# Streaming the tokens of the last product's tiles 2 to 7 in other orders

## The chip, the cores and the metric

The kernel runs on one core of a Trainium2 chip. The metric is the device time of one launch in microseconds (us); lower is better.

## The reference, cut to what matters

Two transformer-like blocks follow each other on 512 tokens of width 1024, all in float32. The change lies in the last product of the second block, the down projection of its feed-forward part. The lines that matter:

```python
ffn = (silu(u2 @ w_ffn_gate) * (u2 @ w_ffn_up)) @ w_ffn_down   # 2816 -> 1024 wide
h = h + gate2 * ffn
return rms_norm_2(h, final_g)
```

## The kernel before

**Layout.** Activations lie transposed: 128 features on the partitions, the 512 tokens side by side in the free dimension. A weight matrix is cut into blocks of 128 x 128. An output tile is 128 features x 512 tokens of float32, which is one whole PSUM bank.

**Precision.** Each float32 operand is split into a rounded part ("hi") and a rest ("lo"), both of a type (fp32r) that TensorE multiplies in one pass. A block is then three matmuls into the same bank: weight hi by activation hi (line 725), weight lo by activation hi (line 726), weight hi by activation lo (line 728). Each is one instruction that holds 128 x 128 weights and streams 512 columns, one for each token. The stationary operand is the weight block; the moving operand is the activation pair `act2`, the product of the two halves of the feed-forward part.

**Weights.** They come in units of eight blocks (512 KB). SyncE's queue loads a unit into `raw`; ScalarE rounds it to `whi` (line 1222); the rest `wlo` is made by VectorE (line 2231, in this stretch) or by ScalarE and a DMA that adds. There are four buffers of each. TensorE's last matmul of a unit frees its buffers.

**The last product.** It has eight output tiles of 22 blocks each. Tiles 1 to 7 (m = 0 to 6 in the loop of `tensor_engine`) go through `tile`, which takes a PSUM bank, calls `block` 22 times and gives the bank back. The banks rotate among eight. VectorE reads each finished tile with all its 512 columns in order and adds it to the residual (line 2459); squares for the norm follow on ScalarE and VectorE. Tile 8 (m = 7) is done apart, in two halves of 256 tokens (lines 1192 to 1194), so that the norm of the first half overlaps the second; sums of squares (lines 1152 and 1162), rows (line 1172), the last scaling (line 2525) and the stores end the kernel.

`taps`, `s5` and the attention part use TensorE for smaller float32 products. One of them, line 910, streams a moving operand that is four runs of 32 columns with gaps between the runs; lines 970 and 979 stream 128 and 127 columns in a row, the latter into PSUM from an odd column on.

Of the kernel before, what the change touches and what calls it, by code (L numbers as in the profile page):

```python
# [13 lines left out]
UB = 8  # L14
NRAW = 4
NHI = 4
NLO = 4
# [90 lines left out]
class Book:  # L108
# [19 lines left out]
    def at(self, *name):  # L128

        return self.events[name] if self.real else self.events.get(name, (None, 0))  # L130
# [85 lines left out]
class Kit:  # L216
# [83 lines left out]
    def sr(self, *name):  # L300

        return self.place(*self.book.home[name])[1]
# [389 lines left out]
def tensor_engine(k, T):  # L692


    at, sb, sr, sm, done = k.at, k.sb, k.sr, k.sm, k.pe_done
    queries = k.queries
    matmul, transpose = T.eng.matmul, T.eng.transpose
# [5 lines left out]
    def take(*tile):  # L703

        i, old = free.pop(0)
        k.bank[tile] = i
        k.book.before[tile] = [old] if old else []
        T.wait_ge(*k.freed(*tile))
        return k.banks[i]

    def give(*tile):
        free.append((k.bank[tile], tile))

    def block(tile, kk, pair, out, start, stop):

        u, j = divmod(len(k.plan), UB)
        k.plan.append((tile[0], kk, tile[1]))
        c = slice(128 * j, 128 * j + 128)
        wh, wl = k.whi[:, u % NHI, c], k.wlo[:, u % NLO, c]
        if u == 0 and j == 0:  # L720
            T.wait_ge(at("w_hi_part"), at("w_lo_part"))
        elif j == 0 or (u, j) == (0, UB // 2):
            T.wait_ge(at("w_hi", u), at("w_lo", u))
        T.wait_ge(at(pair, kk, "hi"))
        matmul(out, wh, sr(pair, kk, "hi"), start=start, stop=False)  # L725
        matmul(out, wl, sr(pair, kk, "hi"), start=False, stop=False)  # L726
        T.wait_ge(at(pair, kk, "lo"))
        mm = matmul(out, wh, sr(pair, kk, "lo"), start=False, stop=stop)  # L728
        if stop or j == UB - 1:
            mm.then_inc(*done.tick(tile if stop else None))  # L730
        if j == UB - 1:
            done.note("unit", u)

    def tile(w, m, ks, pair, norms=()):

        if (w, m) in ready:
            return
        out = take(w, m)
        for kk in ks:
            if norms and kk == ks[-1]:  # L740
                sums(norms, 0)
            block((w, m), kk, pair, out, kk == ks[0], kk == ks[-1])
        give(w, m)
# [26 lines left out]
    def sums(norms, m, first=0, last=7):  # L770


        if m == first:
            take("sums", norms[0])
        b = k.ps("sums", norms[0])
        for i, n in enumerate(norms):
            T.wait_ge(at("sq", n, m) if m == last and n != 1 else at("sq_part", n, m))
            for t in range(4):
                c = 4 * i + t
                mm = matmul(b[:, c:c + 1], sb("sq", n, m)[:, 128 * t:128 * t + 128], k.ones[:, 0:1],  # L780
                            start=m == first and c == 0, stop=m == last and c == 4 * len(norms) - 1)
            mm.then_inc(*done.tick(None, ("sq", n, m)))
        if m == last:
            done.note("sums", norms[0])
            give("sums", norms[0])
# [353 lines left out]
    for j in range(22):  # L1139
        tile("w_ffn_gate_2", j, range(8), "h5")  # L1140
        tile("w_ffn_up_2", j, range(8), "h5")
    done.release(*[("h5", i, h) for i in range(8) for h in ("hi", "lo")])
    for m in range(7):
        tile("w_ffn_down_2", m, range(22), "act2")

    def sums_others(h):

# [1758 lines left out]
def build(nc, *tensors):  # L2906
    with ExitStack() as top:
        k = Kit(nc, top, *tensors)
        layout(k)
        k.edge = k.sb("edge")[:, 0:64].rearrange("p (g e n) -> p g e n", g=4, e=2)  # L2910
        k.ssm_b, k.ssm_c = (k.sb(n).rearrange("p (c s n) -> p c s n", c=c, s=16)
                            for n, c in (("ssm_b", 2), ("ssm_c", 2)))
        k.uk = k.sb("uk").rearrange("p (c n) -> p c n", c=2)
        for real in (False, True):
            k.book.real = real
            for s in k.sigs:
                s.n = 0

            def eng(e):
                return Eng(e if real else Counting())  # L2920

            tensor_engine(k, eng(nc.tensor))
            scalar_engine(k, eng(nc.scalar))
            vector_engine(k, eng(nc.vector))
            gpsimd_engine(k, eng(nc.gpsimd))
            sync_engine(k, eng(nc.sync))
        return k.plan
# [97 lines left out]
```

## Time and profile before

| | |
|---|---|
| median of 3 runs | 1467.01 us (1464.62 to 1467.63) |
| the profiled execution's own time | 1468.92 us |
| its span, first to last instruction | 1467.6 us |
| mean granted TensorE clock | 0.996 of full |
| TensorE matmul busy | 1450.2 us, 99% of the span, 6992 matmuls |
| VectorE / ScalarE / GpSimd busy | 61% / 54% / 12% |

The duration that the profile gives a matmul holds its way through the array, which overlaps the next matmul. What a matmul costs in a stream is the distance from its start to the next one's start.

### The profile page before, as it was taken

The numbers are of one execution on the slowest core, as the hardware profiler recorded it, in microseconds if no ns is written. First come the engines' busy times: TensorE is split into PE (matmuls) and PEld (weight loads), VectorE is DVE, ScalarE is ACT, GpSimd is POOL, SyncE is SP. The second block draws the span as 40 slices with busy tenths as digits, with TensorE's granted clock in tenths as the row PEclk, the third lists the DMA queues.
The fourth block names the chain that finished last, engine by engine and source line by source line (L and its number), as shares of the span: only waits on it lengthen the run. The fifth ranks groups of instructions, "written<-read, shape, count | busy, mean of one in ns | idle before, by whom it ended". The sixth has DMA issues, their size and how long they took to land.

```text
span 1467.6 us, 18322 instructions
## 1 busy us (share of the span) xinstructions
PE 1450.2 (99%) x6992; PEld 1190.5 (81%) x6992; DVE 888.4 (61%) x1623; ACT 787.8 (54%) x1082; POOL 173.0 (12%) x183
## 2 busy tenths in 40 slices
PE   9999999999999999999999999999999999999998
PEld 8887788888888788888888877776878888888887
DVE  6879854365595859476477668847876343333332
ACT  6699898745665556543444565586356222222221
POOL 1111111111111111100002421121010000000000
PEclk9999999999999999999999999999999999999999
DMA  8876888899999798883348666895467433333321
GB/s 260 190 193 161 205 190 200 193 318 292 305 262 273 183 243 224 207 259 122 108 165 280 198 165 167 205 337 201 141 155 222 150 107 109 87 101 100 101 72 58
DMA packets 86935, 275.42 MB, mean 188 GB/s; under 512 B 10096, under 2 KB 14448, under 8 KB 86848
## 3 DMA queue, kind: packets, MB, share of 16 engines
q1 hardware_dynamic: 62256, 190.95, 38.8%
q0 software_dynamic: 21344, 77.67, 27.8%
q10 hardware_dynamic: 3248, 5.64, 1.1%
q8 instruction: 55, 0.90, 0.2%
q14 instruction: 32, 0.26, 0.1%
HBM read 177.62 MB, written 17.83 MB: 133 GB/s over the span
## 4 chain that ended last, share of the span: by engine, by line
PE 86%; ACT 5%; DVE 5%; DMA 2%; issue 1%; SPq 0%; DVEq 0%; ACTq 0%
PE ps L725 27%; PE ps L728 26%; PE ps L726 26%; DMA wlo<-raw 2%; ACT whi L1222 1%; ACT wlo L1231 1%; DVE pl_f L2119 1%; ACT pl_f L1345 1%; PE ps L1071 1%; PE ps L845 0%; PE ps L960 0%; DMA tab<-pl_f 0%; PE ps L979 0%; DVE pl_f L2142 0%; PE ps L834 0%
## 5 line engine op out<-in xcount | busy, mean ns | idle before, releaser
L725 PE MATMUL ps<-pl_r,whi 128*128 128x512 f32 x1954 | 767.3, 393 | 8.4 <-DMA wlo<-raw 4.1
L726 PE MATMUL ps<-pl_r,wlo 128*128 128x512 f32 x1954 | 762.4, 390 | 0.0
L728 PE MATMUL ps<-pl_r,whi 128*128 128x512 f32 x1954 | 762.2, 390 | 0.1
L725 PEld LDWEIGHTS ps<-pl_r,whi 128*128 128x128 f32 x1954 | 367.7, 188 | 91.3 <-issue 7.9
L728 PEld LDWEIGHTS ps<-pl_r,whi 128*128 128x128 f32 x1954 | 367.9, 188 | 77.6 <-DVE pl_r L2168 0.5
L726 PEld LDWEIGHTS ps<-pl_r,wlo 128*128 128x128 f32 x1954 | 367.8, 188 | 75.2 <-issue 0.5
L1222 ACT ACTIVATE whi<-raw 128x1024 fp32r<-128x1024 f32 x246 | 259.3, 1054 | 189.8 <-PE ps L728 149.8
L2541 POOL DMA_DIRECT2D wlo<-raw x148 | 128.4, 868 | 838.0 <-ACT wlo L1231 697.7
L2231 DVE TENSOR_TENSOR wlo<-raw,whi 128x1024 fp32r<-128x1024 f32 x97 | 119.9, 1241 | 92.6 <-ACT whi L1222 92.6
L1231 ACT ACTIVATE wlo<-raw 128x1024 fp32r<-128x1024 f32 x148 | 154.8, 1046 | 0.0
L2495 DVE TENSOR_TENSOR pl_f<-ps,pl_f 128x512 f32<-128x512 f32 x20 | 13.8, 692 | 133.3 <-PE ps L728 133.3
L1683 DVE TENSOR_TENSOR pl_r<-pl_f,pl_r 128x512 fp32r<-128x512 f32 x112 | 77.2, 690 | 9.2 <-ACT pl_r L1251 4.9
L1251 ACT ACTIVATE pl_r<-pl_f 128x512 fp32r<-128x512 f32 x34 | 21.5, 632 | 112.3 <-DVE pl_f L2495 92.9
L1409 ACT ACTIVATE pl_f<-ps,vec 128x512 f32<-128x512 f32 x44 | 33.9, 775 | 61.5 <-PE ps L728 56.5
L2119 DVE CUSTOM_DVE_ANT_0 pl_f<-pl_f,pl_f 128x1024 f32<-128x1024 f32 x48 | 63.1, 1330 | 3.8 <-ACT pl_f L1383 3.8
L1241 ACT ACTIVATE pl_f<-pl_f 128x512 f32<-128x512 f32 x36 | 22.3, 627 | 62.0 <-DVE pl_f L2459 44.3
L1625 ACT ACTIVATE pl_f<-ps 128x512 f32<-128x512 f32 x20 | 11.9, 597 | 58.1 <-PE ps L728 58.1
L2643 POOL TENSOR_TENSOR pl_f<-pl_f,pl_f 128x256 f32<-128x256 f32 x2 | 1.4, 720 | 344.4 <-ACT pl_f L1648 344.4
L2193 DVE SCALAR_TENSOR_TENSOR pl_f<-ps,vec,pl_f 128x511 f32<-128x511 f32 x44 | 32.8, 745 | 12.8 <-ACT pl_f L1409 12.8
L1668 DVE TENSOR_TENSOR pl_f<-pl_f,pl_f 128x512 f32<-128x512 f32 x34 | 23.5, 692 | 19.9 <-ACT pl_f L1241 19.0
L1826 DVE SCALAR_TENSOR_TENSOR pl_f<-pl_f,pl_f 128x512 f32<-128x512 f32 x20 | 12.9, 689 | 34.7 <-ACT pl_f L1357 34.7
L2196 DVE SCALAR_TENSOR_TENSOR pl_f<-ps,vec,pl_f 128x511 f32<-128x511 f32 x44 | 33.0, 750 | 1.5
(300 smaller groups left out, 1180.2 us busy)
## 6 DMA issues: line engine op xcount, KB each, us to landing
raw<-in_w SPq DMA_DIRECT2D x245, 512.0 KB, 4.6
wlo<-raw POOLq DMA_DIRECT2D x148, 512.0 KB, 6.5
pl_f<-in_mod SPq DMA_DIRECT2D x48, 512.0 KB, 7.9
pl_f<-tab SPq DMA_DIRECT2D x12, 512.0 KB, 7.2
xs<-pl_f SPq DMA_DIRECT2D x16, 256.0 KB, 7.9
tab<-pl_f SPq DMA_DIRECT2D x8, 512.0 KB, 6.1
pl_f<-xs SPq DMA_DIRECT2D x16, 256.0 KB, 5.8
spill<-pl_f ACTq DMA_DIRECT2D x16, 256.0 KB, 5.0
```

Source lines behind the costliest of these rows:

```text
L725: matmul(out, wh, sr(pair, kk, "hi"), start=start, stop=False)
L726: matmul(out, wl, sr(pair, kk, "hi"), start=False, stop=False)
L728: mm = matmul(out, wh, sr(pair, kk, "lo"), start=False, stop=stop)
L1222: act(k.whi[:, u % NHI, :], k.raw[:, u % NRAW, :], ACT.Copy).then_inc(*k.w_hi.tick(("w_hi", u)))
L1231: act(k.wlo[:, u % NLO, :], k.raw[:, u % NRAW, :], ACT.Copy, scale=-1.0).then_inc(*k.w_neg.tick(("w_neg", u)))
L1409: act(sb("up", j), ps("w_up", j), ACT.Identity, bias=vc("conv_f_b", j), scale=vc("conv_f_w", 44 + j)).then_inc(*done.tick(("up_tap", j)))
L1683: tt(sr(pair, m, "lo"), src, sr(pair, m, "hi").bitcast(F32), ALU.subtract).then_inc(*done.tick((pair, m, "lo"), *freed_by))
L2119: V.eng.tensor_tensor_reduce(r, r, sb(*c), 1.0, 0.0, ALU.mult, ALU.add, sm("mod", u)).then_inc(*done.tick(("mod_used", u), *([mod_home(u)] ...
L2193: stt(f[:, 1:S], b[:, 0:S - 1], vc("conv_f_w", j), f[:, 1:S], ALU.mult, ALU.add).then_inc(*done.tick())
L2196: stt(f[:, 0:S - 1], b[:, 1:S], vc("conv_f_w", 88 + j), f[:, 0:S - 1], ALU.mult, ALU.add).then_inc(*done.tick(("up", j), ("w_up", j)))
L2231: tt(k.wlo[:, u % NLO, :], k.raw[:, u % NRAW, :], k.whi[:, u % NHI, :].bitcast(F32), ALU.subtract).then_inc(*done.tick(("w_lo", u)))
L2541: P.eng.dma_start(k.wlo[:, u % NLO, :].bitcast(F32), k.raw[:, u % NRAW, :], accum_op=ALU.add).then_inc(*k.w_lo[u % NLO].tick(("w_lo", u)))
```

## The change

In the last product, tiles with m = 1 to 6 get the same matmuls, but the columns of both the output and the moving operand are visited in another order. Since both are reordered alike, each token's result still lands in its own column. For m = 1 the order is backwards. For m = 2 to 6 the 512 columns are seen as a x b x c and visited with b outermost, then a, then c: runs of c neighbouring columns, between which the address jumps.

| m | a, c | b | runs of | runs in a matmul | jump between run starts inside a group |
|---|---|---|---|---|---|
| 2 | 2, 4 | 64 | 4 | 128 | 256 columns |
| 3 | 2, 2 | 128 | 2 | 256 | 256 columns |
| 4 | 8, 8 | 8 | 8 | 64 | 64 columns |
| 5 | 16, 4 | 8 | 4 | 128 | 32 columns |
| 6 | 64, 4 | 2 | 4 | 128 | 8 columns |

The loop over the blocks is written out in place of `tile` and `block`. In it the wait for the activation's lo part stands ahead of the block's first matmul and no longer ahead of its third. Weights, PSUM banks, semaphore steps and all other engines' code are as before.

```diff
+    def streamed(ap, m):
+
+        if m == 1:
+            return ap[:, ::-1]
+        if m > 1:
+            a, c = ((2, 4), (2, 2), (8, 8), (16, 4), (64, 4))[m - 2]
+            return ap.rearrange("p (a b c) -> p b a c", a=a, c=c)
+        return ap
+
     for m in range(7):
-        tile("w_ffn_down_2", m, range(22), "act2")
+        out = take("w_ffn_down_2", m)
+        for kk in range(22):
+            u, j = divmod(len(k.plan), UB)
+            k.plan.append(("w_ffn_down_2", kk, m))
+            c = slice(128 * j, 128 * j + 128)
+            wh, wl = k.whi[:, u % NHI, c], k.wlo[:, u % NLO, c]
+            if j == 0:
+                T.wait_ge(at("w_hi", u), at("w_lo", u))
+            T.wait_ge(at("act2", kk, "hi"), at("act2", kk, "lo"))
+            o, hi, lo = (streamed(ap, m) for ap in (out, sr("act2", kk, "hi"), sr("act2", kk, "lo")))
+            matmul(o, wh, hi, start=kk == 0, stop=False)
+            matmul(o, wl, hi, start=False, stop=False)
+            mm = matmul(o, wh, lo, start=False, stop=kk == 21)
+            if kk == 21 or j == UB - 1:
+                mm.then_inc(*done.tick(("w_ffn_down_2", m) if kk == 21 else None))
+            if j == UB - 1:
+                done.note("unit", u)
+        give("w_ffn_down_2", m)
```

## Rows read from the trace of the kernel before

**Rows 1.** The page: busy time, and the chain that ended last.

```profile
PE 1450.2 (99%) x6992; PEld 1190.5 (81%) x6992; DVE 888.4 (61%) x1623; ACT 787.8 (54%) x1082; POOL 173.0 (12%) x183
...
PE 86%; ACT 5%; DVE 5%; DMA 2%; issue 1%; SPq 0%; DVEq 0%; ACTq 0%
```

**Rows 2.** Stretches (start:end us; length, busy and count by engine, clock, DMA share, GB/s).

```profile
1352.20:1441.90 89.70, 89.70 (x397) 74.26 (x397) 27.49 (x27) 21.76 (x24) 0.00 (x0) 1.00 0.26 76
1442.00:1459.60 17.60, 17.60 (x149) 17.57 (x148) 5.32 (x12) 2.51 (x4) 0.00 (x0) 1.00 0.15 53
22.20:24.40 2.20, 2.20 (x7) 1.74 (x6) 1.59 (x3) 2.20 (x5) 0.00 (x0) 0.51 0.88 269
```

**Rows 3.** Groups by line, 1352.2 to 1441.9 us (busy us, mean ns, idle before).

```profile
L728 PE MATMUL ps<-pl_r,whi 128*128 128x512 f32 x133 | 51.7, 389 | 0.0
L725 PE MATMUL ps<-pl_r,whi 128*128 128x512 f32 x132 | 51.3, 389 | 0.0
...
L726 PEld LDWEIGHTS ps<-pl_r,wlo 128*128 128x128 f32 x132 | 24.8, 188 | 5.1
L2231 DVE TENSOR_TENSOR wlo<-raw,whi 128x1024 fp32r<-128x1024 f32 x16 | 19.6, 1226 | 48.9 <-ACT whi L1222 48.9
L1222 ACT ACTIVATE whi<-raw 128x1024 fp32r<-128x1024 f32 x16 | 16.9, 1058 | 45.9 <-PE ps L728 45.9
L2459 DVE SCALAR_TENSOR_TENSOR pl_f<-ps,sml,pl_f 128x512 f32<-128x512 f32 x6 | 4.5, 750 | 7.2 <-PE ps L728 7.2
```

**Rows 4.** Timeline of TensorE inside tile m = 4 (start us, duration us).

```profile
1399.86 0.39 PE L725 MATMUL ps<-pl_r,whi 128*128 128x512 f32 x1
1400.09 0.39 PE L726 MATMUL ps<-pl_r,wlo 128*128 128x512 f32 x1
1400.32 0.39 PE L728 MATMUL ps<-pl_r,whi 128*128 128x512 f32 x1
1400.54 0.39 PE L725 MATMUL ps<-pl_r,whi 128*128 128x512 f32 x1
```

**Rows 5.** Timeline of VectorE: last act2 rest, then a tile's read.

```profile
1339.31 0.69 DVE L1683 TENSOR_TENSOR pl_r<-pl_f,pl_r 128x512 fp32r<-128x512 f32 x1
...
1367.42 0.75 DVE L2459 SCALAR_TENSOR_TENSOR pl_f<-ps,sml,pl_f 128x512 f32<-128x512 f32 x1 [0.34 <-PE ps L728]
```

**Rows 6.** Timeline of TensorE in the last tile: 256 columns, first and last of 27.

```profile
1449.38 0.28 PE L1192 MATMUL ps<-pl_r,whi 128*128 128x256 f32 x1
...
1452.50 0.28 PE L1194 MATMUL ps<-pl_r,whi 128*128 128x256 f32 x1
```

**Rows 7.** Timeline of TensorE early on, clock granted at half.

```profile
22.58 0.63 PE L728 MATMUL ps<-pl_r,whi 128*128 128x512 f32 x1
23.01 0.63 PE L725 MATMUL ps<-pl_r,whi 128*128 128x512 f32 x1
23.43 0.63 PE L726 MATMUL ps<-pl_r,wlo 128*128 128x512 f32 x1
23.86 0.63 PE L728 MATMUL ps<-pl_r,whi 128*128 128x512 f32 x1
24.29 1.71 PE L845 MATMUL ps<-cst,sml 128*128 128x128 f32 x8
```

**Rows 8.** Timeline of TensorE: gapped runs (910), one run (970), odd start (979).

```profile
493.80 0.67 PE L910 MATMUL ps<-pl_f,pl_f 128*32 128x128 f32 x16
...
812.00 1.08 PE L970 MATMUL ps<-pl_f,pl_f 128*32 128x128 f32 x32
812.90 0.94 PE L979 MATMUL ps<-pl_f,pl_f 128*32 128x127 f32 x28
```

**Rows 9.** Single instructions: durations ns min/median/max of lines 910, 970 and 979.

```profile
L910 PE MATMUL ps<-pl_f,pl_f x64: 272/273/326, 493.8 to 709.1; 128*32 128x128 f32 x64
...
L970 PE MATMUL ps<-pl_f,pl_f x128: 272/273/297, 812.0 to 868.4; 128*32 128x128 f32 x128
...
L979 PE MATMUL ps<-pl_f,pl_f x256: 272/272/272, 812.9 to 870.1; 128*32 128x127 f32 x128
```

## The prediction

> **What bounds the kernel now.** I began with the page. TensorE's matmuls are busy 99% of the span, and the chain that ended last is 86% TensorE [rows 1]; so the question is what TensorE does in the stretch that the diff touches. The reads of finished tiles (line 2459) are six in 1352.2 to 1441.9 us, and the one at 1367.42 us waited for TensorE until just then [rows 3, 5]: this stretch is the six changed tiles, m = 1 to 6. The stretch view gives it 89.70 us at full clock, matmuls busy all through it, 397 of them, one being cut by the window's edge [rows 2]. The diff's count is 6 tiles x 22 blocks x 3 = 396. By both: 89.70 / 396 = 0.2265 us a matmul. The timeline inside a tile says the same: three starts take 1400.54 - 1399.86 = 0.68 us, 0.227 each [rows 4]. By line, their idle time before is 0.0 [rows 3].
>
> So the stretch is bound by the rate at which columns stream, and nothing else is near. VectorE and ScalarE work 27.5 and 21.8 us in the 89.7, ScalarE's rounding of weights waits 45.9 us in total for TensorE to free buffers, and DMA is at 0.26 [rows 2, 3]. Weight loads (188 ns, line 726's as the others') lie beside the matmuls, and 227 - 188 = 39 ns are free on that side [rows 3]. Whatever a matmul of this stretch gains or loses is therefore multiplied by 396 and goes to the end undamped: tile 8 follows back to back [rows 2] and the norm hangs on it.
>
> **The change part by part.** *Instructions.* None is added or removed: 396 matmuls with the same weights, the same columns and the same banks. Nothing to count.
>
> *The earlier wait for the lo part.* The last lo part of `act2` is written at 1339.31 + 0.69 = 1340.0 us [rows 5]. Its first reader is the last block of tile m = 0, which ends about where the stretch begins; the block starts some 3 x 0.227 us before 1352.2, at 1351.5. The wait has been fulfilled for 11 us; it costs 0, and would begin to cost only if the part came 11 us later. The earlier lo parts have more time still, since block 0 reads the oldest. Queued behind the wait is only TensorE itself.
>
> *Readers.* VectorE's read keeps its addresses and its 750 ns; the bank it frees returns only after seven more takes. 0.
>
> *The column order.* This is the whole question: what a matmul of 512 columns costs when both of its streams jump or run backwards. The trace has no fp32r matmul with such streams, so I bound it.
>
> Below: a stream can't beat one column in a cycle of 2.4 GHz. A matmul of 256 columns costs (1452.50 - 1449.38) / 26 = 0.120 us [rows 6], one of 512 costs 0.227; the difference, 0.107 for 256 columns, is 2.4 columns per ns, and 0.120 - 0.107 = 0.013 us is left as a fixed part. If other orders removed that part entirely, the gain would be 396 x 0.013 = 5 us. I know no reason for it: the part isn't a matter of addresses within a row, as it is alike for 256 and 512 columns.
>
> Above: the slowest rate that this trace shows for the same instruction is at half clock, 0.51 granted [rows 2]: four starts in 24.29 - 22.58 = 1.71 us, 0.427 each, one column per cycle of 1.2 GHz [rows 7]. A memory side that delivers two neighbouring columns in one 1.2 GHz step, and falls to one when the neighbours don't come in order, would give just this. The price is 0.427 - 0.227 = 0.200 us a matmul: 66 x 0.200 = 13.2 us a tile, 79.2 us for all six.
>
> Nearest row: line 910, a float32 matmul whose moving operand is four runs of 32 columns with gaps. Sixteen of them take 0.67 us, and the last is 0.27 long: (0.67 - 0.27) / 15 = 27 ns apart. Line 970, the same shape in one run: (1.08 - 0.27) / 31 = 26 ns. Line 979, 127 columns into PSUM from an odd column on: (0.94 - 0.27) / 27 = 25 ns [rows 8]. Single durations are equal, 273, 273 and 272 ns [rows 9]. So jumping in the moving stream every 32 columns costs nothing, and neither does a PSUM stream whose pairs straddle. These products stream slower per column than the fp32r ones (four run side by side, so 4 x 26 = 104 ns for 128 columns, against 53 ns at 2.4 columns per ns) and have longer runs: they speak for zero, but not for runs of 2 at full rate, nor for going backwards. I take 0, keep 5 us below and 79 us above.
>
> At this point two rules of the Trainium skill disagree. PSUM — Partial Sum Buffer, in its Specifications (TRN2), says that any non-contiguous access pattern slows matmuls significantly. Advanced Engine Details and Errata, PSUM Cachelines, repeats it but adds that every two consecutive elements should be contiguous, and its SBUF Cachelines asks for two hits on a line of 16 bytes. Here every regrouped order keeps at least aligned pairs, so by the second form the sum would be 0, by the first something up to the 79 us above. The trace's gapped rows do not reach short runs, so they can't decide between the forms.
>
> **Sum.** 0 + 0 + 0 against the profiled execution: span 1467.6, time 1468.92, so 1.3 us lie around the span. The median of the runs is 1467.0, 1.9 below that execution; I predict the median, 1467.0 us.
>
> **Rivals.**
>
> *Whole or half: all six at one column per 1.2 GHz step.* It needs that only a step of +1 is streamed at the full rate. 1467.0 + 79.2 = 1546 us. For it: contiguous is all that the trace shows of fp32r. Against it: line 910. Chance 0.08. The Trainium skill, PSUM — Partial Sum Buffer, Specifications (TRN2), states what amounts to this rival; line 910's equal spacing [rows 8] speaks against its "any".
>
> *Only the backwards tile halves.* Place: m = 1. Pairs come in the wrong order within their word, and a unit that joins only ascending neighbours splits them. +13.2: 1480 us. No row shows a negative step. Chance 0.12.
>
> *Only the runs of two halve.* Place: m = 3. Each pair lies 256 columns from the one before; if a memory fetches more than 8 bytes at a time, or alternates between halves, then a jump at every pair breaks it, where runs of 4 survive. This decides from c = 2 down. +13.2: 1480 us. Chance 0.09. With the backwards tile as well: +26.4, 1493 us. Chance 0.05.
>
> *A toll for each jump.* One cycle of 2.4 GHz for each run: 128 + 256 + 64 + 128 + 128 = 704 runs x 66 matmuls x 0.417 ns = 19.4 us, 1486 us; m = 3 would bear 7 of them, and m = 1 none. Line 910 has only four runs (1.7 ns by this toll, against a 1 ns reading), so it hardly speaks against it. Chance 0.07.
>
> *The new orders are faster.* The fixed 0.013 us shrinks: down to 1462 us. Chance 0.02.
>
> *The orders never reach the chip* (the patterns simplified away when the program is built): output and operand can't both be flattened, since each is a true permutation. Time as forecast; within its chance.
>
> **How the numbers follow.** No change: 0.57, at 1467.0, own range 1464 to 1470. The rivals above: 0.08 + 0.12 + 0.09 + 0.05 + 0.07 + 0.02 = 0.43. A measurement of this kernel tells 0.2%, 2.9 us, from nothing; all slow cases are beyond it, the faster one mostly. Faster 0.02, within 0.57, slower 0.41. For 8 in 10 the range must take in the single-tile cases and the toll; I let it reach to two slow tiles, 1463 to 1494, and leave out the case of all six and the largest gain.
>
> **What would show it.** The starts in the timeline of each tile: 0.68 us for three in all six tiles says the forecast is right; 1.28 in one tile and 0.68 in the others names the rival by its tile; values between (0.68 + 3 x 0.053 = 0.84 in m = 2, 5 and 6, and 1.00 in m = 3) mean the toll. The six reads by VectorE should lie 14.96 us apart, apart from its own queue. Stalls of TensorE on weights or on `act2` should stay at 0. The prediction is wrong if a short run or a negative step costs at full rate what 32-column runs at a lower rate did not show.

## The result and the profile after

The change makes the kernel slower: 1479.8 us against 1466.3, ratio 1.0083 (95% interval 1.0065 to 1.0101). The forecast was no change, with a chance of 0.57, and that did not happen; the stated range, 1463 to 1494, does hold the time.

The stretch view of the changed kernel, cut at the first start of each tile m = 1 to 6 (start:end, length, TensorE busy and count, clock, DMA share, GB/s):

```profile
1352.33:1367.73 15.40, 15.40 (x67) 1.00 0.31 94
1367.73:1384.23 16.50, 16.50 (x67) 1.00 0.34 95
1384.23:1406.66 22.43, 22.43 (x67) 1.00 0.20 71
1406.66:1422.49 15.83, 15.83 (x67) 1.00 0.28 75
1422.49:1438.78 16.29, 16.29 (x67) 1.00 0.18 57
1438.78:1454.20 15.42, 15.42 (x68) 1.00 0.00 0
```

A straight tile takes 66 x 0.2267 = 14.96 us. Here every tile takes more, at full clock and with TensorE busy throughout: together 101.87 against 89.76, 12.1 us. The spans differ by 1479.8 - 1467.6 = 12.2 us. So the whole loss of the profiled execution lies in these six tiles, and it reaches the end undamped. (The medians differ by 13.5 us; by the interval of the ratio the loss is 9.5 to 14.8.) The stretch begins where it did, at 1352.3 us against 1352.2.

The groups by line in m = 3 (MATMUL streams columns, LDWEIGHTS loads a block) and the timeline in m = 1, then in m = 3:

```profile
L1165 PE MATMUL ps<-pl_r,whi 128*128 128x512 f32 x23 | 11.7, 508 | 0.0
...
L1164 PEld LDWEIGHTS ps<-pl_r,wlo 128*128 128x128 f32 x22 | 4.3, 197 | 3.0
L2257 DVE TENSOR_TENSOR wlo<-raw,whi 128x1024 fp32r<-128x1024 f32 x3 | 3.7, 1225 | 16.0 <-ACT whi L1248 16.0
```

```profile
1352.33 0.40 PE L1163 MATMUL ps<-pl_r,whi 128*128 128x512 f32 x1
1352.56 0.40 PE L1164 MATMUL ps<-pl_r,wlo 128*128 128x512 f32 x1
1352.80 0.40 PE L1165 MATMUL ps<-pl_r,whi 128*128 128x512 f32 x1
1353.03 0.40 PE L1163 MATMUL ps<-pl_r,whi 128*128 128x512 f32 x1
...
1395.10 0.51 PE L1165 MATMUL ps<-pl_r,whi 128*128 128x512 f32 x1
1395.44 0.51 PE L1163 MATMUL ps<-pl_r,whi 128*128 128x512 f32 x1
1395.78 0.51 PE L1164 MATMUL ps<-pl_r,wlo 128*128 128x512 f32 x1
1396.12 0.51 PE L1165 MATMUL ps<-pl_r,whi 128*128 128x512 f32 x1
```

Three starts take 0.70 us in m = 1 and 1.02 in m = 3, where [rows 4] have 0.68. TensorE never idles before a matmul in this stretch; VectorE waits for ScalarE and that for TensorE as in [rows 3]. By (start of the next tile - start of this one) / 66 a matmul costs, in ns:

| m | 0 | 1 | 2 | 3 | 4 | 5 | 6 |
|---|---|---|---|---|---|---|---|
| order | straight | backwards | runs of 4 | runs of 2 | runs of 8 | runs of 4 | runs of 4 |
| cost | 226.7 | 233.3 | 250.0 | 339.8 | 239.8 | 246.8 | 233.3 |
| loss of the tile, us | 0 | 0.4 | 1.5 | 7.5 | 0.9 | 1.3 | 0.4 |

m = 4 isn't even: its first nine blocks cost between about 235 and 263 ns a matmul, all later ones 233.3. (In m = 6 the cost is that of blocks 1 to 21.)

All costs below are read in this way from the starts in each kernel's timeline. The starts are given to 0.01 us, so the cost in a whole tile is good to about 0.2 ns and that in one block of three matmuls to about 3 ns. Thirteen kernels are told of; each leaves everything outside the loop of the last product as it is, except the last one. Ten of them ran once. Their loops begin anywhere from 1333.3 to 1341.3 us, so of these kernels only the costs inside the tiles are used, and not the whole time.

### The profile page after: what moved, and what is told of

The parts are those of the page before. It is cut to its first block, busy times and chain, and to the rows that moved or that the text cites. A ratio compares the mean times of both kernels' runs of the same rounds, so it can differ in the third digit from the quotient of the medians.

```text
span 1479.8 us, 18323 instructions
## 1 busy us (share of the span) xinstructions
PE 1462.8 (99%) x6992; PEld 1191.8 (81%) x6992; DVE 888.6 (60%) x1623; ACT 787.6 (53%) x1082; POOL 172.7 (12%) x183
## 4 chain that ended last, share of the span: by engine, by line
PE 88%; DVE 5%; ACT 4%; DMA 2%; issue 1%; DVEq 0%; ACTq 0%
PE ps L725 25%; PE ps L728 24%; PE ps L726 24%; PE ps L1164 3%; PE ps L1163 3%; PE ps L1165 3%; DMA wlo<-raw 1%; ACT whi L1248 1%; DVE pl_f L2145 1%; ACT wlo L1257 1%; PE ps L1071 1%; DMA tab<-pl_f 1%; PE ps L960 0%; PE ps L845 0%; ACT pl_f L1371 0%
## 5 line engine op out<-in xcount | busy, mean ns | idle before, releaser
L725 PEld LDWEIGHTS ps<-pl_r,whi 128*128 128x128 f32 x1800 | 338.9, 188 | 84.9 <-issue 8.0
L728 PEld LDWEIGHTS ps<-pl_r,whi 128*128 128x128 f32 x1800 | 338.9, 188 | 72.5 <-DVE pl_r L1709 0.9
L726 PEld LDWEIGHTS ps<-pl_r,wlo 128*128 128x128 f32 x1800 | 339.0, 188 | 69.1 <-issue 0.5
L2219 DVE SCALAR_TENSOR_TENSOR pl_f<-ps,vec,pl_f 128x511 f32<-128x511 f32 x44 | 32.8, 746 | 14.0 <-ACT pl_f L1435 14.0
```

## The experiments

### Which of the two streams pays

`mov_only` and `out_only` keep the six orders for one side alone:

```diff
-            o, hi, lo = (streamed(ap, m) for ap in (out, sr("act2", kk, "hi"), sr("act2", kk, "lo")))
+            o, hi, lo = (out, *(streamed(ap, m) for ap in (sr("act2", kk, "hi"), sr("act2", kk, "lo"))))  # mov_only
+            o, hi, lo = (streamed(out, m), sr("act2", kk, "hi"), sr("act2", kk, "lo"))                    # out_only
```

> The six orders on the moving operand alone; the output is written straight, so the tokens of tiles 2 to 7 land in wrong columns (this part of the result is changed). After the change a matmul cost 233, 250, 340, 240, 247 and 233 ns in m = 1 to 6 against 227 straight. Theory S, the reads from SBUF pay: the same six numbers here. Theory P, the accumulating writes to PSUM pay: 227 in all six. Theory B, a part of each: the runs of two (m = 3) show between 227 and 340, and what is missing shows in the kernel with the output alone.

> The six orders on the output alone, the moving operand straight; tokens of tiles 2 to 7 land in wrong columns (this part of the result is changed). Theory S: 227 ns a matmul in all six tiles. Theory P: 233, 250, 340, 240, 247, 233. Theory B: numbers between, which add up with those of the kernel with the moving operand alone to the 7, 23, 113, 13, 20 and 7 ns of the change.

Timeline of `mov_only` inside m = 3:

```profile
1395.00 0.51 PE L1165 MATMUL ps<-pl_r,whi 128*128 128x512 f32 x1
1395.34 0.51 PE L1163 MATMUL ps<-pl_r,whi 128*128 128x512 f32 x1
1395.68 0.51 PE L1164 MATMUL ps<-pl_r,wlo 128*128 128x512 f32 x1
```

and of `out_only` inside m = 3:

```profile
1384.86 0.39 PE L1165 MATMUL ps<-pl_r,whi 128*128 128x512 f32 x1
1385.09 0.39 PE L1163 MATMUL ps<-pl_r,whi 128*128 128x512 f32 x1
1385.32 0.39 PE L1164 MATMUL ps<-pl_r,wlo 128*128 128x512 f32 x1
```

0.34 us from start to start in the one, 0.23 in the other. Over all tiles `mov_only` has 233, 250, 340, 240, 247 and 233, `out_only` 226.7 in all six. Theory S holds without remainder: the moving operand, which is read from SBUF, pays everything, the reordered writes to PSUM nothing.

### Whether the tiles add up

```diff
-        if m == 1:
-            return ap[:, ::-1]
-        if m > 1:
+        if m == 3:                 # pairs_alone; no_pairs returns ap for m == 3 instead
             a, c = ((2, 4), (2, 2), (8, 8), (16, 4), (64, 4))[m - 2]
```

> The change with only the order of m = 3 (runs of two) taken back. Its 66 matmuls cost 340 - 227 = 113 ns more each, 7.5 us. If the costs of the tiles are independent and go to the end undamped, the time falls by 7.5 us below the change, to about 1472, +0.3% against before. Rival: the slow tile disturbs those after it (m = 4 began at 250 and fell to 233 after nine blocks), then m = 4 shows 233 from its first block and the time falls by another 0.4 us.

> Only m = 3 is reordered (runs of two, 256 apart); the other tiles stream straight. Its 66 matmuls cost 340 instead of 227 ns: +7.5 us, so +0.51% against before, about 1474. Rival, that the tiles' costs are not additive: m = 4, now straight behind it, starts above 227 ns for many blocks and the sum is more.

`no_pairs` took 1471.8 us, ratio 1.0033 (1.0019 to 1.0046); `pairs_alone` 1475.0, ratio 1.0055 (1.0033 to 1.0077). Forecast were +0.3% and +0.51%. In `pairs_alone` m = 3 costs 339.7 ns and the tile behind it 227.3; the losses of the two kernels, 7.5 us for `pairs_alone` and 4.5 us for `no_pairs` by their tiles, lie within what their ratios allow. In `no_pairs` m = 4 did not start at 233: it is above it for five blocks (237.7 on the mean) where it was for nine. Its slow start needs no slow tile ahead.

> Output and moving operand alike: runs of 8, 64 apart (order A) in m = 0, 1, 3, 5, 6; runs of 4, 256 apart in m = 2; straight in m = 4. In the change A began at about 250 ns and fell to 233 after nine blocks, behind tile m = 3; with m = 3 straight it fell after five. If A relaxes from a state that another order left: m = 0 relaxes, m = 1 is 233 from its first block, m = 3 relaxes again behind m = 2, m = 5 behind the straight tile too, m = 6 is 233 throughout. If it hangs on the operands' addresses: the first nine blocks are slow in all five tiles.

```diff
+        a, c = ((8, 8), (8, 8), (2, 4), (8, 8), (1, 1), (8, 8), (8, 8))[m]
+        return ap.rearrange("p (a b c) -> p b a c", a=a, c=c) if a > 1 else ap
```

Order A (runs of 8, 64 apart): m = 0 relaxes within five blocks (some 260, 243, 267, 257 and 237 ns, then 233), m = 1 is at 233 from its start, m = 3 relaxes within nine, m = 5 within five, m = 6 is at 233 throughout. So the slow start hangs on what streamed before and not on the operands' addresses: the same order, streamed again, settles into a cheaper rhythm.

### Which orders cost what

> Seven tiles, output and moving operand alike, two halves 256 columns apart, runs of 2, 4, 8, 16, 32, 64 and 128 columns in m = 0 to 6. Toll theory (each jump costs a fixed time once the fixed 7 ns are paid; 106.7 ns for 256 runs is 0.417 ns each): 340, 287, 260, 247, 240, 237, 235. Against it stands m = 2 of the change, runs of 4 at 250. Threshold theory (runs of two fall out of a window that runs of four nearly fit): 340, 250, then 233 to 227 for all longer runs.

```diff
+        return ap.rearrange("p (a b c) -> p b a c", a=2, c=2 ** (m + 1))
```

Measured: 339.7, 250.3, 243.3, 240.0, 236.7, 227.0 and, for runs of 128, 227 in each block. Both theories fail: from runs of 4 to runs of 32 each doubling takes off some 3 to 7 ns, so it is no fixed toll for a jump, and no threshold behind 4 either.

> Output and moving operand alike, runs of 4 columns; groups of 2, 4, 8, 16, 32, 64 runs that lie 256, 128, 64, 32, 16 and 8 columns apart in m = 0 to 5; in m = 6 runs of 4 taken in descending order. Known from the change: 256 apart 250 ns, 32 apart 247, 8 apart 233. If the small cost hangs on the distance of the jump, it falls in steps: 250, 250, 247, 247, 240, 233, and 233 in m = 6. If it hangs on how many jumps there are, all are 250, since each order has 128 runs; m = 5 of the change speaks against that already. A toll for the way back (the jump to the next group) would make it rise from m = 5 to m = 0 with the number of groups 2, 4, 8, 16, 32, 64: 233 to 250, a doubling of the part over 233 at each step.

```diff
+        if m == 6:
+            return ap.rearrange("p (b c) -> p b c", c=4)[:, ::-1]
+        return ap.rearrange("p (a b c) -> p b a c", a=2 ** (m + 1), c=4)
```

Measured: 250, 268, 278, 247, 227, 233 and 233. Same runs, same number of jumps, and the cost neither falls with the distance nor rises with the number of groups. None of the three readings holds.

> Only the moving operand is reordered, in all seven tiles (tokens of tiles 1 to 7 land in wrong columns, this part of the result is changed). m = 0, 1, 2: steps of 2, 4, 8 columns; m = 3: single columns taken in turn from the two halves; m = 4: neighbours swapped (1, 0, 3, 2); m = 5: pairs swapped inside each four (2, 3, 0, 1); m = 6: fours swapped (4 to 7, 0 to 3). Theory L, a fetch brings a line of four columns and each new line costs at least 3 cycles of 2.4 GHz (256 runs of two: 768 cycles + 48 = 816 = 340 ns): m = 0 two columns from each line: 340; m = 1, 2, 3 one from each: (1536 + 48) / 2.4 = 660; m = 4, 5, 6 four from each line: 233 to 250. Theory R, only the length of ascending runs counts, wherever they lie: 660 for m = 0 to 4, 340 for m = 5, 250 for m = 6. Theory W, the fetch is two columns wide: 660 for m = 0 to 3, 233 for m = 4, 233 to 340 for m = 5.

```diff
+        if m < 3:
+            return ap.rearrange("p (b a) -> p a b", a=2 ** (m + 1))
+        if m == 3:
+            return ap.rearrange("p (a b) -> p b a", a=2)
+        if m == 4:
+            return ap.rearrange("p (b a) -> p b a", a=2)[:, :, ::-1]
+        if m == 5:
+            return ap.rearrange("p (b a c) -> p b a c", a=2, c=2)[:, :, ::-1]
+        return ap.rearrange("p (b a c) -> p b a c", a=2, c=4)[:, :, ::-1]
```

Timeline of `line_hits`, in m = 0 (steps of 2), then in m = 3 (single columns in turn from two halves):

```profile
1344.92 0.64 PE L1168 MATMUL ps<-pl_r,whi 128*128 128x512 f32 x1
1345.38 0.63 PE L1166 MATMUL ps<-pl_r,whi 128*128 128x512 f32 x1
1345.83 0.63 PE L1167 MATMUL ps<-pl_r,wlo 128*128 128x512 f32 x1
1346.28 0.63 PE L1168 MATMUL ps<-pl_r,whi 128*128 128x512 f32 x1
...
1429.87 0.38 PE L1166 MATMUL ps<-pl_r,whi 128*128 128x512 f32 x1
1430.09 0.38 PE L1167 MATMUL ps<-pl_r,wlo 128*128 128x512 f32 x1
1430.30 0.38 PE L1168 MATMUL ps<-pl_r,whi 128*128 128x512 f32 x1
1430.52 0.38 PE L1166 MATMUL ps<-pl_r,whi 128*128 128x512 f32 x1
```

0.453 us in the one and 0.216 in the other. Steps of 2, 4 and 8: 453, 461, 431. Neighbours swapped and pairs swapped inside fours: 227, as straight; fours swapped: 233. And the order with the most jumps of all is cheaper than straight, 216. No theory had that.

> Only the moving operand is reordered, in seven tiles (their tokens land in wrong columns, this part of the result is changed): single columns in turn from two neighbouring blocks of 128, 64, 32, 16, 8, 4 and 2 columns in m = 0 to 6. So two columns that follow each other in the stream lie that far apart, 512 bytes down to 8. Known: 256 apart, 216 ns; steps of 2, 4 and 8 columns through the row, 453, 461 and 431 ns. Theory D, two successive columns are fetched together, and in one step only where they lie in one small word or in different banks: from some distance down the cost jumps from 216 to some 430 to 460. Theory U, what counts is that both halves of each 8-byte word are used soon after each other (the step orders return to a word only after a whole sweep): 216 to 227 at all seven distances.

> Only the moving operand is reordered, in seven tiles (their tokens land in wrong columns, this part of the result is changed). m = 0 to 3: single columns in turn from 4, 8, 16 and 32 equal parts of the row. m = 4 and 6: in turn from two halves, but in steps of 2 and of 4 columns inside each, in as many sweeps. m = 5: in turn from two halves, the second half first. Theory D: m = 0 216 or a little more (neighbours in the stream 512 bytes apart), m = 4, 5, 6 216, since each pair still lies 256 columns apart. Theory U: m = 4 and 6 some 430 to 460, m = 5 216.

```diff
+        return ap.rearrange("p (g a b) -> p g b a", a=2, b=128 >> m)        # distance
+        if m < 4:                                                           # turns
+            return ap.rearrange("p (a b) -> p b a", a=4 << m)
+        if m == 5:
+            return ap.rearrange("p (a b) -> p b a", a=2)[:, :, ::-1]
+        return ap.rearrange("p (a b s) -> p s b a", a=2, s=2 if m == 4 else 4)
```

`distance`: 215.8 at 128, 64, 32, 16, 8 and 4 columns, 227 at 2; theory D, which wanted a rise to 430 or more, fails and U holds. `turns`: 283, 488, 433 and 433 from 4 to 32 parts; halves in steps of 2 cost 227, in steps of 4 451; second half first 215.8. Now U fails too: with steps of 2, 8-byte words are visited again only after a sweep, and yet it costs 227. The number of lines visited isn't it either. Steps of 2, and halves in steps of 2, both make 256 visits to a line of four columns and take two columns at each, and they cost 453 and 227.

The orders so far fall into groups, with two exceptions, once the stream is thought of as dealt to two readers, columns 1, 3, 5, ... to the one and 2, 4, 6, ... to the other, and one asks how many columns in a row each takes from one line of four columns (16 bytes). Two halves in turn: four. Straight, swapped neighbours, distance 2, halves in steps of 2: two. Steps of 2 and more, many parts: one. This was fitted to the numbers after the fact.

| in a row, for each reader | orders | ns |
|---|---|---|
| four | in turn from two places, 4 to 256 columns apart | 216 |
| two | straight, swaps, backwards, runs of 4 and more | 227 to 278 |
| one | steps of 2, 4, 8, many parts | 431 to 488 |
| one, two lines in rotation | runs of 2 from two halves; singles from four parts | 340; 283 |

Two runs put this to the test.

> Only the moving operand is changed, in seven tiles, and in five of them it doesn't even hold all tokens (columns of tiles 1 to 7 of the last product are wrong, this part of the result is changed). The theory that stands, T: every other column of the stream (1st, 3rd, ... and 2nd, 4th, ...) is read by a reader of its own, each with a line of 16 bytes (four columns) of its own; four columns that a reader takes in a row from one line cost 216 ns a matmul, two 227 and a little more when lines jump, one 430 to 490. m = 0, each of the first 256 columns twice in a row: four in a row for each reader, 216. m = 1, each fourth column four times: two, 227 to 250. m = 2, each eighth column eight times: four, 216. m = 3, each fourth column twice, the whole twice over: one, 430 to 490. m = 4, in turn from fours, the eights descending: four, 216. m = 5, in turn from two halves, descending: four, 216 where plain descending costs 233. m = 6, one column 512 times: 216. Rival H, what counts is how many successive columns of the stream share a line, by one reader: m = 0 and 3 (two different addresses a line, two hits each): both alike; m = 1 and straight alike, 227. In m = 3 H gives what it gives for steps of 2, where two successive columns share a line too, 453, and m = 0 227.

```diff
+        if m == 0:
+            return ap[:, 0:256].unsqueeze(2).broadcast_to([128, 256, 2])
+        if m == 1:
+            return ap[:, ::4].unsqueeze(2).broadcast_to([128, 128, 4])
+        if m == 2:
+            return ap[:, ::8].unsqueeze(2).broadcast_to([128, 64, 8])
+        if m == 3:
+            return ap[:, ::4].unsqueeze(2).unsqueeze(1).broadcast_to([128, 2, 128, 2])
+        if m == 4:
+            return ap.rearrange("p (g a b) -> p g b a", a=2, b=4)[:, ::-1]
+        if m == 5:
+            return ap.rearrange("p (a b) -> p b a", a=2)[:, ::-1]
+        return ap[:, 0:1].broadcast_to([128, 512])
```

Timeline of `repeats`, in m = 0 (each column twice in a row), then in m = 3 (each fourth column twice):

```profile
1339.77 0.38 PE L1171 MATMUL ps<-pl_r,wlo 128*128 128x512 f32 x1
1339.98 0.38 PE L1172 MATMUL ps<-pl_r,whi 128*128 128x512 f32 x1
1340.20 0.38 PE L1170 MATMUL ps<-pl_r,whi 128*128 128x512 f32 x1
1340.41 0.38 PE L1171 MATMUL ps<-pl_r,wlo 128*128 128x512 f32 x1
...
1390.04 0.63 PE L1170 MATMUL ps<-pl_r,whi 128*128 128x512 f32 x1
1390.49 0.63 PE L1171 MATMUL ps<-pl_r,wlo 128*128 128x512 f32 x1
1390.94 0.63 PE L1172 MATMUL ps<-pl_r,whi 128*128 128x512 f32 x1
1391.39 0.63 PE L1170 MATMUL ps<-pl_r,whi 128*128 128x512 f32 x1
```

Measured: 215.8, 227.6, 215.8, 450.9, 216.2, 215.8, 217. All seven as T had them, within 1 ns where it named a single value. What decides against rival H is m = 0, with 216 where H had 227, and that m = 0 and m = 3 are far from alike. That m = 3 costs 451, though two successive columns are even the same one, both had; by T it is because each reader gets one column from a line.

> Only the moving operand is reordered (tokens of tiles 1 to 7 land in wrong columns, this part of the result is changed): runs of two in turn from 4, 8, 16, 32, 64 and 128 equal parts of the row in m = 0 to 5; single columns from 64 parts in m = 6. With two parts it was 340 (the m = 3 of the change). By theory T each reader gets one column from a line before it must go to another, so T with a single line for each reader gives 430 to 490 for all seven, and can't say why two parts cost only 340 and single columns from four parts 283. T with room for two lines: two parts should have been as cheap as straight, so 340 speaks against that as well; if lines are held for a while, the cost rises with the number of parts in the rotation, from 340 over 4 parts to 430 to 490 at 16 and more, and m = 6 is 433 as with 16 and 32 parts. Against T altogether would be any of these at 250 or less.

```diff
+        a, c = (4 << m, 2) if m < 6 else (64, 1)
+        return ap.rearrange("p (a b c) -> p b a c", a=a, c=c)
```

Measured: 444, 487, 461, 431, 461, 451 and, for single columns, 431. All seven lie within what a single line for each reader gives, already at four parts. The two cases with exactly two lines in rotation, 340 and 283, stay between; how a reader gains from them isn't explained.

### A kernel that uses it

> The kernel before, with the moving operand read in turns from the two halves of the row in 1422 matmuls: tiles 1 to 7 of the last product (462) and the gate and up products of the second block from j = 2 on (960). The output is written straight, and its readers on ScalarE and VectorE read PSUM in steps of two to put the tokens back. If the 216 ns hold: 1422 x 10.6 ns = 15.1 us less, 1452, -1.0%. Rival: the readers' steps of two in PSUM slow them so far that TensorE waits for a bank; they have several us of slack in each 5.4 us of a pair of tiles, so they would have to take over three times as long. Rival: 216 ns holds only in the line_hits kernel, by what ran beside it: no change.

```diff
+def turned(ap):
+    return ap.rearrange("p (a b) -> p b a", a=2)     # also: ordered "p (a b) -> p a b", unturned "p (b a) -> p a b"
+
+        if in_turns(tile):                           # in block(): gate and up from j = 2, the last product
+            hi, lo = turned(hi), turned(lo)
...
-            act(sb("f2", j), ps("w_ffn_gate_2", j), ACT.Silu).then_inc(
+            act(ordered(sb("f2", j)), unturned(ps("w_ffn_gate_2", j)), ACT.Silu).then_inc(
...
+            f2 = ordered(sb("f2", j))
+            tt(f2, unturned(ps("w_ffn_up_2", j)), f2, ALU.mult).then_inc(
...
+        if in_turns((w, m)):                         # in gated_add
+            x, y = ordered(x), unturned(y)
```

It took 1453.1 us against 1468.8 of the kernel before on the same chip, ratio 0.9896 (0.9879 to 0.9913): 15.7 us less where 15.1 were forecast. It beats both kernels. Its groups by line from 1340 us on, the same view from 1130 to 1430 us (ScalarE's read of the gate tiles), and the timeline inside the gate and up products:

```profile
L748 PE MATMUL ps<-pl_r,whi 128*128 128x512 f32 x131 | 49.6, 379 | 0.0
...
L2485 DVE SCALAR_TENSOR_TENSOR pl_f<-ps,sml,pl_f 128x512 f32<-128x512 f32 x7 | 5.2, 750 | 10.4 <-PE ps L751 10.4
```

```profile
L1648 ACT ACTIVATE pl_f<-ps 128x512 f32<-128x512 f32 x19 | 11.3, 597 | 53.3 <-PE ps L751 53.3
```

```profile
1299.96 0.38 PE L749 MATMUL ps<-pl_r,wlo 128*128 128x512 f32 x1
1300.18 0.38 PE L751 MATMUL ps<-pl_r,whi 128*128 128x512 f32 x1
1300.39 0.38 PE L748 MATMUL ps<-pl_r,whi 128*128 128x512 f32 x1
1300.61 0.38 PE L749 MATMUL ps<-pl_r,wlo 128*128 128x512 f32 x1
```

VectorE's read of a tile in steps of two in PSUM takes 750 ns, as straight [rows 3], and ScalarE's 597, as its line 1625 did before (597). VectorE's product over the up tiles takes 691 ns (line 2522) against 692 (line 2495 before). So the first rival falls: TensorE never waits for a bank in these products. The readers' slack was larger than the expectation says, as a pair of tiles takes 48 x 0.2267 = 10.9 us and not 5.4. There are 0.65 us for three starts also away from the last product; the second rival falls too.

## Why the prediction was wrong, point by point

*What bounds the kernel, and the factor of 396.* Right. The loss of the tiles, 12.1 us, is that of the span, 12.2.

*The earlier wait, the readers, the instructions: 0.* Right. m = 0, with the new code and the straight order, costs 226.7 ns, and no idle time appears.

*The column order: 0.* This is the step that failed: a cost was put at nothing that measures 12.1 us, 7.5 of them in m = 3. It was priced by line 910, whose 32-column runs cost nothing [rows 8]. For fp32r the runs showed 236.7 ns against 227 with runs of the same length taken in turn from two halves (`run_sweep`), and in the change 250 and 340 with runs of 4 and 2. The prediction itself named the reservation, that the row streams slower per column (104 ns for 128 columns against 53). It is a likely reason why line 910 shows no cost, since a slower stream leaves the reads from SBUF more time; no run here streams the same order at both rates, so this is not shown. The row should have stood as one that can't see the cost, and the value taken should have been above 0. The row on PSUM from an odd column wasn't needed: the output side costs nothing in any of these orders.

*The bounds.* The upper one for all six orders, +0.200 us a matmul, was never reached by an order of the change; steps of 2, 4 and 8 lie above it (+0.226, +0.235 and +0.204), so it bounds nothing in general. The lower one, 0.013 us of gain, was rightly put aside for these six orders, none of which was faster. But the ground given, that this part isn't a matter of addresses within a row, was wrong: reading in turns takes away 0.011 of it.

*The rivals.* Runs of two as the costly tile was right in the place and not in the price: 7.5 us instead of 13.2, and not alone. Backwards costs 0.4 us, not 13.2. The toll for each jump had the size of m = 3 nearly right (7.0 us forecast, 7.5 measured), but m = 2, 5 and 6, with 128 runs each, cost 23, 20 and 7 ns and not 53 each, and `run_sweep` and `jump_sweep` exclude a fixed toll. That the time lies inside the range, and near the 1480 us of a single tile at half rate, is luck: six tiles lost different amounts that happen to add up to 12.1 us, near the 13.2 of a rival that did not occur.

*The two rules cited.* The Trainium skill, PSUM — Partial Sum Buffer, Specifications (TRN2), says that any non-contiguous pattern slows matmuls significantly; `out_only` contradicts the "any": 226.7 ns with backwards and with runs of 2, 4 and 8. Single-column steps of the output were not tried. Line 910, which the prediction set against this rule, says nothing on it: its gaps are in the moving operand, and it writes PSUM in one run of 128 columns. The Trainium skill, Advanced Engine Details and Errata, SBUF Cachelines, asks for two hits on a line of 16 bytes: the numbers agree with two as the border between 227 and 431 or more only if hits are counted for every other column of the stream; steps of 2, with two successive hits, cost 453.

*What stays open.* It is not known why orders with two columns in a row spread over 227 to 278, nor why some settle only over several blocks; the two cases of two lines in rotation, 340 and 283, one of which makes up most of the change's loss (m = 3), are not explained by the model either. That the cost lies in the order of the moving operand is shown; that there are two readers is a model that forecast the seven orders of `repeats` and, in its form with one line for each reader, the seven of `pair_groups`, and not something that a trace shows directly.

## What to carry to other kernels

The order in which an fp32r matmul streams its moving operand has a price of its own; read it as start-to-start distance, by tile. Where the order runs in pieces, keep them long: runs of 2 in turn from two halves cost 340 ns, of 64 and more 227. A row of a product that streams slower did not tell the cost at full rate here. If TensorE is the bound, let the moving operand come in turn from two halves, write PSUM straight and let the reader of PSUM put the tokens back: 227 becomes 216 ns, 1.0% of this kernel's time for a quarter of its 512-column matmuls.

## What the runs showed of the hardware that was not expected

- A moving operand read in turns from two places is faster than one read straight: 215.8 against 226.7 ns for 512 columns, for any distance from 4 to 256 columns.
- In some orders a matmul's cost depends on what streamed before it, for up to nine blocks (27 matmuls), and the same way again in another tile: runs of 8 behind a straight tile went from some 260 to 233 ns in five blocks, twice in `history`.
- Steps of 8 columns (431 ns) cost less than steps of 2 or 4 (453 and 461).
- Matmuls that write PSUM backwards or in runs of 2, 4 or 8 (226.7 ns), and reads of PSUM in steps of two on VectorE (750 ns) and ScalarE (597 ns), cost nothing measurable here.
